# All six units of the first stage's last quarter of h multiplied with split weights, and the modulation pieces dealt anew

## The reference

```
cond = silu(c)
for l in range(2):
    mod = cond @ w_mod[l] + b_mod[l]                 # 2048 -> 12288
    sh1, sc1, g1, sh2, sc2, g2 = split(mod, 6)
    h = rms_norm(x) * (1 + sc1) + sh1
    y = attention(h @ w_attn_in) @ w_attn_out   if l == 0 else pool_mixer(h)
    x = x + g1 * y
    h = rms_norm(x) * (1 + sc2) + sh2
    x = x + g2 * conv_ffn(h, w_up[l], w_down[l])
return rms_norm(x)
```

## Time and profile before

| what | value |
|---|---|
| median of 3 runs | 2056.68 us (2055.4 to 2058.42) |
| the profiled execution's own time | 2053.86 us |
| its span | 2052.3 us |
| PE busy | 97% of the span |
| DVE busy | 81% |
| ACT busy | 52% |
| moved | 560 MB, 273 GB/s in the mean |

### The profile page before, as it was taken

The page is one execution under the profiler, slowest core; times in us unless marked ns, Lnnn a source line. Parts: engine busy times, 40 slices in busy tenths (PEclk is TensorE's granted clock), DMA queues, the critical chain, the costliest instruction groups (busy, mean ns, idle before and its releaser), DMA issues.

```text
span 2052.3 us, 29791 instructions
## 1 busy us (share of the span) xinstructions
PE 1983.3 (97%) x10760; PEld 1708.4 (83%) x10760; DVE 1662.2 (81%) x2190; ACT 1062.4 (52%) x1561; POOL 272.7 (13%) x459
## 2 busy tenths in 40 slices
PE   3999999998999999999999999899999999999998
PEld 3878989887888888888788887688888888888886
DVE  5786899897899999999989987889965666656766
ACT  4323764554655545565446565555543555434553
POOL 3343342220111111111111100011100000000000
PEclk8999999999999999999999999999999999999999
DMA  9999899895789899998999874397756555555563
GB/s 361 367 358 333 303 331 337 302 322 212 272 316 324 312 380 350 322 327 312 349 372 326 306 263 155 109 329 267 253 199 195 194 186 186 195 194 186 189 198 125
DMA packets 236128, 560.04 MB, mean 273 GB/s; under 512 B 14056, under 2 KB 15064, under 8 KB 235352
## 3 DMA queue, kind: packets, MB, share of 16 engines
q1 hardware_dynamic: 180696, 356.86, 50.2%
q0 software_dynamic: 55296, 201.35, 27.5%
HBM read 556.07 MB, written 2.10 MB: 272 GB/s over the span
## 4 chain that ended last, share of the span: by engine, by line
PE 81%; DVE 8%; issue 4%; DMA 4%; ACT 2%; POOL 0%; DVEq 0%; ACTq 0%; POOLq 0%
PE ps L777 27%; PE ps L782 14%; PE ps L801 9%; PE ps L803 9%; PE ps L802 9%; PE ps L837 3%; DVE w_lo L1612 3%; DMA mraw<-in_w_mod 2%; PE ps L752 2%; PE ps L753 2%; PE ps L754 2%; PE ps L834 1%; DVE macc L1641 1%; DVE macc L1626 1%; ACT w_hi L1212 1%
## 5 line engine op out<-in xcount | busy, mean ns | idle before, releaser
L1212 ACT ACTIVATE w_hi<-raw 128x1024 fp32r<-128x1024 f32 x640 | 671.2, 1057 | 745.5 <-PE ps L777 262.0
L1612 DVE TENSOR_TENSOR w_lo<-raw,w_hi 128x1024 fp32r<-128x1024 f32 x640 | 766.4, 1223 | 269.0 <-ACT w_hi L1212 268.2
L777 PE MATMUL ps<-h_pair,w_hi 128*128 128x512 f32 x2816 | 685.2, 393 | 7.2 <-DVE w_lo L1612 6.0
L777 PEld LDWEIGHTS ps<-h_pair,w_hi 128*128 128x128 f32 x2816 | 516.6, 189 | 114.1 <-issue 15.3
L782 PEld LDWEIGHTS ps<-h_pair,w_lo 128*128 128x128 f32 x2816 | 361.0, 191 | 13.9
L782 PE MATMUL ps<-h_pair,w_lo 128*128 128x256 f32 x2816 | 365.2, 283 | 0.0
L801 PE MATMUL ps<-w_hi,g_hi 128*128 128x512 f32 x824 | 324.4, 394 | 0.2
L803 PE MATMUL ps<-w_hi,g_lo 128*128 128x512 f32 x824 | 320.9, 389 | 0.0
L802 PE MATMUL ps<-w_lo,g_hi 128*128 128x512 f32 x824 | 320.7, 389 | 0.0
L1641 DVE SCALAR_TENSOR_TENSOR macc<-mraw,cond,macc 128x1024 f32<-128x1024 f32 x180 | 230.3, 1281 | 30.3 <-DMA mraw<-in_w_mod 22.6
L1626 DVE SCALAR_TENSOR_TENSOR macc<-mraw,cond,macc 128x512 f32<-128x512 f32 x284 | 195.7, 746 | 28.5 <-DMA mraw<-in_w_mod 20.7
(11 more groups left out here) (194 smaller groups left out, 1584.4 us busy)
## 6 DMA issues: line engine op xcount, KB each, us to landing
mraw<-in_w_mod POOLq DMA_DIRECT2D x358, 512.0 KB, 6.2
raw<-in_w_up SPq DMA_DIRECT2D x176, 1024.0 KB, 6.3
raw<-in_w_down SPq DMA_DIRECT2D x88, 1024.0 KB, 5.8
raw<-in_w_attn_in SPq DMA_DIRECT2D x48, 1024.0 KB, 8.6
raw<-in_w_attn_out SPq DMA_DIRECT2D x16, 1024.0 KB, 7.2
work<-in_w_mod POOLq DMA_DIRECT2D x12, 512.0 KB, 8.8
early<-in_w_mod POOLq DMA_DIRECT2D x8, 512.0 KB, 12.2
raw<-in_w_pool SPq DMA_DIRECT2D x4, 1024.0 KB, 5.2
```

Source lines behind the costliest of these rows:

```text
L777: i = mm(ps[:, bank + t, :], w_hi[:, s, kk, t * P:(t + 1) * P], h_pair[:, k, :, :].rearrange("p a t -> p (a t)"), start=first and half == ...
L1212: return nc.scalar.activation(o, i, f, **kw)
L1612: V.tensor_tensor(w_lo[:, s, :, :], raw[:, j % 4, h * 1024:(h + 1) * 1024].rearrange("p (k n) -> p k n", k=2), w_hi[:, s, :, :].bitcast(F3 ...
```

## The change

The three native units of the last quarter, positions 18, 19 and 20, become split units like 21, 22 and 23. Their splits are started where the first stage's preparation ends (18 and 19) and at position 18 (20). The places of the split units in the four slots of `w_hi` and `w_lo`, and the counts that loads and splits wait for, follow. `native(pos)` and `split_number(u)` are new. The free time `FREE[pos]` in the deal of modulation pieces is now one formula for positions 18 to 58, which gives less to positions 18 to 20.

After the change the deal is 2, 1, 2, 1, 1, 2 pieces at positions 18 to 23 and 2, 2, 2, 4, 2, 4, 3, 2 at 24 to 31; counted up to position 23 these are 9 and no longer 13 pieces, up to 31 they are 30 and no longer 34, up to 38 50 and no longer 52, and from 51 on nearly the same. At 54 and 55 it gives 0 and 2, before 2 and 0. The sums of chunks 8 to 16 stand at 25, 28, 31, 34, 38, 41, 43, 46, 49.

```diff
-    H0 = START
+    H0 = 18
@@
+        def native(pos):
+            return pos < 18 and pos % 6 < 3
+
+        def split_number(u):
+            return u - 9 if u >= 18 else 3 * (u // 6) + u % 6 - 3
+
         def split_at(q, j):
             u = 4 * q + j
             if isinstance(u, int) and u < START:
-                n = 3 * (u // 6) + u % 6 - 3
-                return 2 * n, 2 * n
+                n = split_number(u)
+                return 2 * n, 2 * n + 2
             return 8 * q + 2 * j - H0, 2 * j
 
         def slots_used(q, j, h):
             u = 4 * q + j
             if isinstance(u, int) and u < START:
-                n = 3 * (u // 6) + u % 6 - 5
-                return None if n < 0 else 2 * (6 * (n // 3) + 3 + n % 3) + h + 1
+                n = split_number(u) - 2
+                return None if n < 0 else 2 * (n + 9 if n >= 9 else 6 * (n // 3) + 3 + n % 3) + h + 1
             return 8 * q + 2 * j + h - 3
@@
         for pos in range(POS0, 59):
-            own = 6.9 if pos < 21 else 5.6
-            own -= (1.4 if pos < START else 0.0) + (2.45 if pos > 18 else 0.0)
+            own = 5.6 - (1.4 if pos < START else 0.0) - 2.45
@@ SP, load
-                    if u % 6 >= 3:
+                    if not native(u):
                         sp.wait_ge(lo_ready, split_at(u // 4, u % 4)[0] + 2)
                     else:
                         sp.wait_ge(sub_used, 2 * u + 2)
@@ PE, start_unit
-                if pos % 6 < 3:
+                if native(pos):
                     unit_raw(pos)
@@ ACT and DVE, behind the last modulate and h_rest of the first stage
+            start_split(18)
+            start_split(19)
@@ ACT and DVE, loop over positions from 18 on
-                if START - 3 <= pos + 2 < 65:
+                if POS0 + 2 <= pos + 2 < 65:
                     split((pos + 2) // 4, (pos + 2) % 4)
```

## The result

The changed kernel takes 2060.39 us in the median of 13 runs (2056.74 to 2064.4), the kernel before, in the same sessions, 2055.26 (2053.09 to 2059.62). The ratio is 1.0023 [1.0016, 1.003], so the change costs 4.7 us. The forecast was 2052.1, a gain of 4.6. The profiled execution took 2056.74 us with a span of 2055.1; it is the fastest of the thirteen, so its trace shows somewhat less of the loss than the median does.

What follows compares the result with a forecast made beforehand. PE was taken to bound the front, DVE's order of work positions 25 to 35. Terms -3.6 - 1.7 + 0.7 = -4.6 us took 2056.68 to 2052.1 us, range 2049.0 to 2055.4.

Steps and rivals of the forecast that it cites:

- The PE work removed: Positions 18 to 20: split units replace native ones, taking 3.6 us off PE, on the path.
- 5.2 us by passes alone: Units 18 to 20: three products save a quarter of 20.78 us; as a rival 2050.5 us, chance 0.02.
- The new splits in time: Positions 18 to 20: unit 18's split ready 2.4 us before PE starts, first half 3.5; cost nothing, at worst 1 us.
- Loads and queues: Loads of units 22 to 24 come 9 to 14 us earlier, modulation pieces are issued later; cost zero, gain zero.
- Positions 25 to 36: Positions 25 to 35: old PE waits go, DVE gets 2.0 us more; net -1.7 us, bounds -3.7 to +0.3.
- The waits at 27, at 33 and at 35: PE's softplus wait, a head's output wait and chunk 12's sum wait, 1.2 us each, all counted as gone.
- From 36 on: Positions 32 to 50: DVE's 5.3 us of owed pieces fit into its 11 us of free time; cost zero.
- the wait at 59: ACT's 1.3 us moved from 54 to 55 delay the split; PE stalls 0.7 us, between 0 and 1.3.
- the sums' new positions: Chunk 12's sum moves to 38, three positions behind its last piece, so its 1.2 us PE wait goes.
- the deal eats its own gain: Positions 25 to 35: later pieces prolong DVE's chain, old waits return; -1.5 to -3.8 us, 2054 us, chance 0.36.
- The one on the slower side: Positions 27 and 29: four DVE pieces wait some 3 us each for landings, +12 us, 2064 us, chance 0.04.
- the short wait for `mraw`: Position 27: DVE wants piece (10,2) at 239.9 us, it lands about 240.6; +0.7 us.

Runs made afterwards that it cites:

- e2: The kernel before, keeping its three native units at 18 to 20, with only the new deal of pieces; median 2063.14 us, ratio 1.0022.
- e4: The changed kernel with the pieces of positions 54 and 55 exchanged, so they stand as before; median 2060.85 us, ratio 1.0015.
- e5: The changed kernel with chunk 13's sum moved from ahead of unit 41 to between its halves; median 2059.48 us, ratio 1.001.
- e8: The changed kernel with ACT's first pieces of chunks 12 and 17 one position later (33 and 48); median 2056.08 us, ratio 0.9997.
- e6: The changed kernel with 3,2,2,2,2,2 pieces at 18 to 23, old deal to 31, then 2,1,2,2, new deal from 36; 2053.9 us, ratio 0.9993.
- e12: The changed kernel with first pieces of chunks 12 and 17 later, chunk 13's sum inside unit 41, 54 and 55 exchanged; 2054.64 us, ratio 0.9995.
- e3: Kernel before with six split units, 3,2,2,2,2,2 pieces at 18 to 23 and the old deal from 24; 2052.6 us, ratio 0.9967.
- e7: Kernel before with six split units, 3,2,2,2,2,2 pieces at 18 to 23, pieces further ahead at 24 to 34, old deal from 35; 2053.95 us, ratio 0.9993.

## Why the prediction was wrong

**The PE work removed: right.** Units 18, 19 and 20 became shorter by 3.69 us (forecast 3.6). The Trainium skill ("FP8 and Floating Point Precision", TensorE Precision Notes) gives four passes to a true 32-bit product. The estimate of 5.2 us by passes alone is not borne out by the trace, which has 3.69.

**The new splits in time: right.** DVE in order of time around the end of the preparation:

```profile
164.94 2.36 DVE L1619 TENSOR_TENSOR w_lo<-raw,w_hi 128x1024 fp32r<-128x1024 f32 x2
168.40 1.23 DVE L1619 TENSOR_TENSOR w_lo<-raw,w_hi 128x1024 fp32r<-128x1024 f32 x1 [1.10 <-ACT w_hi L1217]
171.06 1.23 DVE L1619 TENSOR_TENSOR w_lo<-raw,w_hi 128x1024 fp32r<-128x1024 f32 x1 [1.43 <-ACT w_hi L1217]
```

The first half of 18 is done at about 166.2 and PE takes it at 169.8, 3.6 us later (forecast 3.5). No unit from 18 to 23 waits. Loads and queues cost nothing.

**Positions 25 to 36: right in the main, two terms missing.** The waits at 27, at 33 and at 35 went, as forecast; that at 32 grew from 0.87 to 2.30 us (forecast 1.9). A wait of 0.65 at 34 had been left out. And behind the wait at 32 the clock fell, which I had not priced. PE in order of time:

```profile
265.79 0.67 PE L1005 MATMUL ps<-work 128*128 128x256 f32 x2 [2.30 <-DVE mods L1654]
...
266.75 0.50 PE L807 MATMUL ps<-w_lo,h_pair 128*128 128x512 f32 x1
267.05 0.63 PE L808 MATMUL ps<-w_hi,h_pair 128*128 128x512 f32 x1
...
270.04 0.52 PE L806 MATMUL ps<-w_hi,h_pair 128*128 128x512 f32 x1
270.39 0.39 PE L807 MATMUL ps<-w_lo,h_pair 128*128 128x512 f32 x1
```

and the same time as two stretches; the granted clock stands ahead of the DMA share:

```profile
266.44:270.04 3.60, 3.60 (x13) 2.78 (x11) 3.60 (x5) 1.50 (x3) 2.04 (x5) 0.56 0.95 311
270.04:273.61 3.57, 3.57 (x16) 2.95 (x15) 3.54 (x7) 0.00 (x0) 2.04 (x15) 0.96 1.04 392
```

For 3.4 us PE runs at 1.2 GHz, half its 2.4. Matmuls begin 0.43 us apart and no longer 0.23; for eight of them that is 1.6 us. Set against like work, -4.69 plus the owed sum of 0.89 is -3.8 at unit 36, for a forecast of -5.3: 1.5 short, about the size of that stretch. That the rest agrees is in part luck: the wait at 34, with its slow start 0.9 us, was made up for by old waits that gave back more than their gaps.

**The step that failed is "From 36 on".** It reads: "PE had no idle time there ..., DVE has 136.5 - 125.4 = 11 us free, and since PE never waited there, the catch-up ... fits unless it bunches ... Cost zero." It measured +9.2 us from unit 36 to 63, and +8.3 without the sum that was owed at 36. Of these, 0.85 is the wait at 59, which had a term of its own (0.7). The other 7.5 were priced at nothing. The first table's steps place the 8.3, the sums set aside, and the runs that keep the new deal from 36 on can be put beside it (us lost against the kernel before, one trace each; e2, e4 and e5 share its deal up to 53):

| kernel | 37 to 39 | 41 | 42 to 50 | 51 | 52 to 58 | 59 |
|---|---|---|---|---|---|---|
| after | 3.8 | 2.0 | 0.0 | 1.7 | 0.0 | 0.9 |
| e2, native units | 4.1 | 0.8 | 0.0 | 1.1 | 0.0 | 0.9 |
| e4, 54 and 55 exchanged | 2.3 | 0.1 | 0.8 | 1.7 | 0.3 | 0.0 |
| e5, sum inside 41 | 5.2 | 0.0 | 2.1 | 1.7 | 0.0 | 0.9 |
| e8, first pieces later | 3.0 | 0.5 | 0.0 | 1.2 | 0.1 | 0.9 |
| e6, four pieces fewer at 32 to 35 | 0.8 | 0.0 | 0.0 | 0.7 | 0.0 | 0.9 |
| e12, three places mended | 3.4 | 0.0 | 0.0 | 0.3 | 0.0 | 0.0 |

The first four rows show how far traces of one deal lie apart; only what stands outside them is an effect of an edit. I see three reasons. The runs that take away the first two are clearly faster than the changed kernel; the third rests on traces alone:

1. *DVE is late, and the mean hid it.* The catch-up itself hardly bunches: the new deal has 14 pieces at 32 to 36 for 12, and 14 at 37 to 41 as before. But from 32 to 36 DVE works no more than before, 35.64 of 39.92 us for 36.26 of 39.79, and from 37 to 41 it works 36.80 for 33.98: what it was dealt, it does later. The old stretches:

```profile
267.50:307.29 39.79, 36.55 (x201) 31.57 (x201) 36.26 (x53) 31.59 (x43) 15.79 (x29) 1.00 0.96 341
307.29:343.76 36.47, 36.47 (x298) 36.10 (x298) 33.98 (x55) 19.16 (x32) 9.85 (x14) 1.00 0.95 340
```

With four pieces fewer at 32 to 35 (e6), 37 to 39 cost 0.8 us and not 2.3 to 5.2, and with the old deal from 24 on (e3) no wait behind 35 is left. Moving chunk 12's first piece alone (e8, e12) leaves 3.0 and 3.4. How much of the lateness comes out of the fours at 27 and 29, and how much from what is dealt at 32 to 35, no run tells.

2. *First pieces stand next to the last but three.* Piece (12, 0) may be issued only when (11, 4) is used up. The new deal puts it at 32, right behind, and (17, 0) at 47. ACT in order of time:

```profile
267.58 0.36 ACT L1217 ACTIVATE g_hi<-ps 128x256 fp32r<-128x256 f32 x1
273.94 1.33 ACT L1217 ACTIVATE macc<-mraw,cond 128x512 f32<-128x512 f32 x2 [6.00 <-DMA mraw<-in_w_mod]
275.18 1.99 ACT L1217 ACTIVATE w_hi<-raw 128x1024 fp32r<-128x1024 f32 x2
...
389.92 1.34 ACT L1217 ACTIVATE macc<-mraw,cond 128x512 f32<-128x512 f32 x2 [7.21 <-DMA mraw<-in_w_mod]
391.16 1.99 ACT L1217 ACTIVATE w_hi<-raw 128x1024 fp32r<-128x1024 f32 x2
```

Behind the waiting piece stand the split of `pos + 2` and the next head's steps, and DVE's `w_lo` waits for ACT's `w_hi`. Moving just these two ACT pieces by one position was worth 4.50 - 0.94 = 3.6 us in the trace (e8), 0.95 of it ahead of unit 36; of single places the wait at 34 is gone, which all four traces of the deal have; at 41 and 51 e8 lies within what these four show. The ratio fell from 1.0023 to 0.9997. Landing was not slower where this began: from 215 to 300 us a piece took 6.0 us in the middle and 7.0 at most, for 6.1 and 8.3. Further on it was, from 320 to 335 us, ahead of the sum of point 3: 7.5 in the middle and 9.3 at most, before 6.2 and 6.4. After, first from 215 to 300 us, then from 320 to 335:

```profile
DMA to landing us min/median/max: 4.0/6.0/7.0
...
DMA to landing us min/median/max: 6.0/7.5/9.3
```

3. *The place of a sum is not free.* I counted the sums' new positions as a gain and looked at their distance from the last piece alone. But `mod_sum` writes into the bank of a head's output, and waits for `o_lo` if a head has been written there. The new deal puts chunk 13's sum at 41, right behind head 7's output at 40:

```profile
336.91 0.39 PE L967 MATMUL ps<-tri,nls 128*128 128x128 f32 x2
339.01 1.02 PE L860 MATMUL ps<-ones,macc 128*128 128x1 f32 x8 [1.71 <-DVE g_lo L1847]
```

and DVE in order of time:

```profile
331.93 1.41 DVE L1633 SCALAR_TENSOR_TENSOR macc<-mraw,cond,macc 128x512 f32<-128x512 f32 x2 [1.64 <-DMA mraw<-in_w_mod]
333.26 2.35 DVE L1619 TENSOR_TENSOR w_lo<-raw,w_hi 128x1024 fp32r<-128x1024 f32 x2
...
338.44 0.42 DVE L1847 TENSOR_TENSOR g_lo<-ps,g_hi 128x256 fp32r<-128x256 f32 x1 [1.32 <-ACT g_hi L1217]
```

DVE, late by its pieces and one landing, gives `g_lo` at 338.8, and PE stands until then ahead of unit 41, though nothing is near that needs the sum. The wait needs that lateness: e4 has the sum at the same place and loses 0.1 us there. e5 takes the wait away, but half of the gain comes back one position on and the rest by 50; with e8's edit as well (e12) nothing comes back: the step from 40 to 41 is +0.89, the bare sum, and none follows. No timed run tells this term alone.

**The size of waits.** I priced a wait by its gap. Each costs more: the step at 59 is 0.85 us for a gap of 0.60, at 39 1.19 for 0.95, at 41 2.85 for 1.71 and a sum of 0.89. That is 0.25 us a wait, and makes the 6.2 us of gaps behind 36 (seven, all but those at 32 and 34) into 6.2 + 7 x 0.25 = 8.0, near the 8.3 measured. Most of it lies in how the trace counts: in an unbroken row each matmul of 512 columns is listed with 0.39 us but the next begins 0.23 later, and a gap is counted from the end of the 0.39, so 0.16 us of standing still are not in it.

**The rivals.** The first, that the deal eats its own gain, pointed the right way but ended with position 35. The one on the slower side had its place at the fours of 27 and 29, where DVE was to wait for landings. There it waits for none; the short wait for `mraw` that the forecast had at 27 (0.7 us) did not come either. The mechanism does occur, but at ACT and at the first pieces of 32 and 47, and it needs no slow landing, only a piece wanted sooner than 6 us after its slot came free. The 0.05 for slower left out everything behind 36, as "From 36 on" had priced it at nothing.

**Open.** Why the clock fell behind the wait at 32: every trace with the new deal's places there, and no other, has a stretch of half clock that begins at 265 to 271 us, and e7 one behind its 2.99 us wait; but stretches of 3.4 us also come at unit 3 in six traces of fourteen, with no cause that I varied (ahead of them, in all traces, PE has 2.6 us of matmuls of 8 columns and of one). Taking away only the wait at 32 under the new deal was not tried. Nor was it followed why one deal waits so differently from trace to trace between 34 and 41.

## What to carry to other kernels

When work is moved into a stage in which an engine has free time in the mean, walk through the positions where it arrives one at a time, with the waits of every engine that shares the order (here ACT's first pieces, and the guard of a bank that a sum shares with another result). A consumer placed within one landing of the event that frees its slot holds up everything its engine has behind it; moving two of them by one position, at no cost in work, was worth 3.6 us in the trace, as much as the split units. And an optimization and a new schedule that come together should be timed apart: here the first gave 3.6 us and the second took 8. And several traces of one kernel are needed before a step of 2 us is put down to a cause.

## What the runs showed of the hardware

- Around the end of PE waits of 2.3 to 3.0 us and behind it (seven traces) the granted clock was at half for 3.4 us, 1.6 us of extra time in the trace of after. Behind e7's wait of 2.13 us and e5's of 1.72 it was not; e4 has such a stretch behind 1.28 and 1.22 us, close together. In the wait of 5.3 to 5.5 us at unit 64, which every trace has, the one of before too, it fell to half and stayed there for 6.8 us.
- A PE wait costs about 0.25 us more than its gap in the trace (steps of 0.85, 1.19 and 2.85 us at 59, 39 and 41 for gaps of 0.60 and 0.95, and of 1.71 with a sum of 0.89).
- Three products of the rounded kind take 17 to 18% less time than one native product of 32-bit tiles (18.78 us for 22.47, with the same 1.69 us of logits in both).
